# The experts' second matrix loaded with two neighbouring rows to a partition

## What is computed

```python
def expert_block(args):
    xb, e = args
    hid = xb @ w1[e] + b1[e]
    return clamped_swiglu(hid[:, :D_FF], hid[:, D_FF:]) @ w2[e] + b2[e]
```

## Time and profile before

| | before |
|---|---|
| median of 3 runs | 1869.51 us (1869.2 to 1870.19) |
| profiled execution, first to last instruction (span) | 1867.9 us |
| mean granted TensorE clock in it | 0.955 of 2.4 GHz |
| TensorE busy in the span | 1709.2 us (92%) |
| HBM read in it | 540.33 MB, of which the experts 384 loads of 1024 KB |
| expert loads under way | from 239.61 us to about 1222 us of the span |

### The profile page before, as it was taken

How to read it: one execution, slowest core, us unless ns; L and a number is a source line. 1 busy time by engine, 2 the same in 40 slices (tenths; PEclk the granted TensorE clock), 3 DMA queues, 4 the chain that set the end, 5 groups by cost and what they waited for, 6 DMA issues and landing times.

```text
span 1867.9 us, 20656 instructions
## 1 busy us (share of the span) xinstructions
PE 1709.2 (92%) x8372; PEld 1038.5 (56%) x8372; DVE 470.4 (25%) x1013; ACT 278.9 (15%) x572; POOL 131.5 (7%) x265
## 2 busy tenths in 40 slices
PE   6999999699967989598979789899999999999997
PEld 3644684144332534143434234377877888888886
DVE  4545422021111212021112112234566312121101
ACT  3114322011010111010011011022314300200000
POOL 5780000000000000000000000010003000000000
PEclk7999899899987989699999999999999999999999
DMA  9566089999999999999999999973443335525340
GB/s 377 184 234 229 25 353 370 397 413 414 418 421 416 412 419 419 420 414 412 418 422 416 413 419 418 407 290 113 157 159 113 113 114 202 203 90 180 117 176 24
DMA packets 134211, 547.03 MB, mean 293 GB/s; under 512 B 9195, under 2 KB 21111, under 8 KB 98268
## 3 DMA queue, kind: packets, MB, share of 16 engines
q1 hardware_dynamic: 129248, 529.83, 71.5%
q0 software_dynamic: 4128, 14.42, 2.1%
q10 hardware_dynamic: 732, 1.38, 0.2%
HBM read 540.33 MB, written 7.62 MB: 293 GB/s over the span
## 4 chain that ended last, share of the span: by engine, by line
PE 54%; DMA 15%; SPq 14%; issue 1%; DVE 0%; ACT 0%; DVEq 0%
SPq L1714 14%; PE PS L1337 10%; DMA arena<-in_w 9%; PE PS L2279 8%; DMA ring<-in_w 6%; PE PS L1362 5%; PE PS L2118 4%; PE PS L2305 4%; PE PS L2131 3%; PE PS L2139 3%; PE PS L1313 2%; PE PS L2125 2%; PE PS L1373 2%; PE PS L2269 2%; PE PS L2147 1%; PE PS L1347 1%
## 5 line engine op out<-in xcount | busy, mean ns | idle before, releaser
L1337 PE MATMUL PS<-ring,arena 128*64 128x512 f32 (+2 forms) x960 | 297.5, 672 | 58.0 <-DMA arena<-in_w 38.3
L1337 PE MATMUL PS<-arena 128*32 128x512 f32 (+2 forms) x968 | 269.9, 674 | 28.6 <-DMA ring<-in_w 20.3
L1337 PEld LDWEIGHTS PS<-ring,arena 128*64 128x64 f32 (+2 forms) x960 | 85.9, 141 | 204.2 <-issue 204.0
L1362 PE MATMUL PS<-ring,arena 128*64 128x512 f32 (+2 forms) x528 | 154.3, 620 | 12.5 <-DMA arena<-in_w 8.6
L1337 PEld LDWEIGHTS PS<-arena 128*32 128x32 f32 (+2 forms) x968 | 79.4, 141 | 137.5 <-issue 137.3
L2279 PE MATMUL PS<-arena,ring 128*128 128x256 f32 x704 | 152.6, 379 | 0.0
L1605 DVE TENSOR_SCALAR arena<-PS 128x512 f32<-128x512 f32 x28 | 19.3, 691 | 504.2 <-PE PS L1347 504.2
L2279 PEld LDWEIGHTS PS<-arena,ring 128*128 128x128 f32 x704 | 133.5, 190 | 18.0
L1362 PE MATMUL PS<-arena 128*32 128x512 f32 (+2 forms) x424 | 112.9, 630 | 23.1 <-DMA ring<-in_w 14.7
L1362 PEld LDWEIGHTS PS<-ring,arena 128*64 128x64 f32 (+2 forms) x528 | 47.5, 135 | 87.2 <-issue 86.2
L2118 PE MATMUL PS<-arena,ring 128*128 128x256 f32 x384 | 84.8, 380 | 0.0
(11 more groups left out here) (466 smaller groups left out, 2132.4 us busy)
## 6 DMA issues: line engine op xcount, KB each, us to landing
ring<-in_w SPq DMA_DIRECT2D x186, 1024.0 KB, 23.1
arena<-in_w SPq DMA_DIRECT2D x174, 1024.0 KB, 22.9
ring<-in_w_ada SPq DMA_DIRECT2D x24, 1024.0 KB, 9.5
cst<-in_w SPq DMA_DIRECT2D x24, 1024.0 KB, 23.8
ring<-in_w_in SPq DMA_DIRECT2D x22, 1024.0 KB, 7.3
ring<-in_w_up SPq DMA_DIRECT2D x20, 1024.0 KB, 8.9
ring<-in_w_gate SPq DMA_DIRECT2D x16, 1024.0 KB, 6.4
ring<-in_w_down SPq DMA_DIRECT2D x11, 1024.0 KB, 8.2
```

Of the source, the lines that this page charges most:

```text
L1337: m = pe.matmul(bank(("up", i, b))[rows[n], :], xs[:, k, rows[n]], tiles[n][:, b * 512:(b + 1) * 512], start=k == 0, stop=False, skip_grou ...
L1362: m = pe.matmul(bank(("down", i, c))[rows[n], :], actT[:, k, rows[n]], tiles[n][:, a:a + 512], start=k == 0, stop=k == 7, skip_group_check ...
```

## The change

A piece of `w2` is now read as one run: partition p gets rows 2p and 2p + 1 of the 256, which are neighbours in HBM, so 8 KB come in one piece and the DMA has the shape 128 x 2048 instead of 128 x 2 x 1024. The slot's half a now holds the rows 2p + a. So that the features still meet their rows, the transposes of a group of 256 features take every second column: even ones for the first half, odd ones for the second. The sums are the same.

```diff
 def __init__(self, slot, fill, after, src, m, n, rank=None, added=0):
-        self.added = added
+        self.added, self.paired = added, False
...
     def expert(self, key, src, m, n, rank, slot=None):
         self.weights[key] = (m, [self.load(src, m, n, rank, slot)])
+        self.loads[-1].paired = m > 1
...
                         for j in range(4):
-                            m = pe.transpose(bank(("flip", i, c), j * 128, (j + 1) * 128), um[c][:, j * 128:(j + 1) * 128], ident)
+                            half = um[c][:, j // 2 * 256:j // 2 * 256 + 256].rearrange("t (f a) -> t a f", a=2)
+                            m = pe.transpose(bank(("flip", i, c), j * 128, (j + 1) * 128), half[:, j % 2, :], ident)
...
-                    sp.dma_start(v, one.src.rearrange("(k p) n -> p k n", p=128)).then_inc(filled[one.slot], 16)
+                    if one.paired:
+                        sp.dma_start(v.rearrange("p k n -> p (k n)"), one.src.rearrange("(p k) n -> p (k n)", p=128)).then_inc(filled[one.slot], 16)
+                    else:
+                        sp.dma_start(v, one.src.rearrange("(k p) n -> p k n", p=128)).then_inc(filled[one.slot], 16)
...
-                    sp.dma_start(v, one.src[bass.ds(known[one.rank], 1), :, :].rearrange("e (k p) n -> p (e k) n", p=128)).then_inc(filled[one.slot], 16)
+                    src = one.src[bass.ds(known[one.rank], 1), :, :]
+                    if one.m > 1:
+                        sp.dma_start(v.rearrange("p k n -> p (k n)"), src.rearrange("e (p k) n -> p (e k n)", p=128)).then_inc(filled[one.slot], 16)
+                    else:
+                        sp.dma_start(v, src.rearrange("e (k p) n -> p (e k) n", p=128)).then_inc(filled[one.slot], 16)
```

## The result

The changed kernel takes 1859.13 us (median of four runs, 1855.82 to 1863.16) against 1869.36 us for the kernel before beside it (1868.87 to 1870.19): a ratio of 0.9943, with a 95% interval of 0.9926 to 0.996. The forecast was 1860.9 us with a range of 1859.2 to 1864.5; the median lies 1.8 us under the forecast and 0.07 us under the lower end of the range. The profiled execution is one of 1859.9 us, with a span of 1858.1 us and a mean granted clock of 0.961.

What follows compares the result with a forecast made beforehand. The prediction took the experts' stage to be bound by its stream of 384 loads. 126 `w2` loads at 0.069 us gave 8.6 us, transposes and stream loss zero: 1869.5 - 8.6 = 1860.9 us, range 1859.2 to 1864.5.

Steps and rivals of the forecast that it cites:

- neither grows nor shrinks: From 1226 us on, behind the experts' stage: TensorE's 642 us only move with the stage's end.
- The stage lasts as long as its loads: Experts' stage, to about 1225 us: its 384 loads set its length; TensorE waits 125.1 us for them.
- the 116 forecast: Experts' stage: TensorE's waits for DMA were to be near 125 - 9 = 116 us after the change.
- 126 x 0.069 = 8.6: Experts' stage: 126 `w2` loads each gain 0.069 us at `w1`'s rate, 8.6 us; upper bound 9.4, lower bound zero.
- I take no loss: At 420 to 470 us: the stream gets 1.5 us further ahead, within its 1.9 us margin; otherwise 7.1 us gained.
- a sign of being wrong: At about 420 to 470 us: a DMA share below 1 would show the prediction wrong.
- The likeliest case: Whole kernel: the forecast itself, 7.1 to 9.4 us gained, 1859.6 to 1862.9 us, chance 0.79.
- part of it: Stream runs dry where TensorE has no gap, or form explains only part of the rate: 1863 to 1866, chance 0.10.
- The end of the stage: Last `w2` matmuls: last eight loads come 0.55 us sooner, 0.84 of 1.39 us waiting stays; the end follows the last load.
- The transposes: Ahead of `down`, eight to a unit, 112 in all: reading every second column costs zero, at most 1.15 us a unit.
- my upper bound of 144 ns more: Weight load of a transpose, 128 columns, 141 ns before: most that the step of two could add, from line 500.
- The rule of line rate: Experts' loads: by the skill, full rate from 512 bytes on, so no gain, 1869.5 us; the windows disagreed.

Runs made afterwards that it cites:

- e1_again: The changed kernel as it is, timed again beside the kernel before: 1858.56 us, ratio 0.9944.
- e5_before_again: The kernel before, unchanged, timed against itself: 1868.39 us, ratio 1.0006.
- e3_load_only: The changed kernel with the old transposes, so only the loads are new: 1859.49 us, ratio 0.9952 of the kernel before.
- e4_half_units: Loads and transposes changed in units 0 to 6 only, the rest as in the kernel before: 1865.17 us, ratio 0.9977.
- e6_w1_4k: The changed kernel with `w1` of units 1 to 13 read as 256 pieces of 4 KB: 1878.31 us.
- e2_turn_only: The kernel before with the strided transposes alone and the old loads: 1867.0 us, ratio 0.9992.
- e10_pieces: Loads alone, all computing left out, `w1` streamed in sections: 387, 410, 422 and 428 GB/s at pieces of 2, 4, 8 and 16 KB.
- e7_w2_2k: The changed kernel with `w2` of units 1 to 13 read as 512 pieces of 2 KB: 1890.54 us.

## Why the prediction was right in its steps, and where it failed

**The step that failed** is the one that put the time outside the stage at a constant: what follows the stage "neither grows nor shrinks", the part ahead of it got no term at all, and the range allowed for "runs that spread by half a microsecond either way". That was read off three runs of the kernel before, 1869.2 to 1870.19. The runs showed something else. In the thirteen traces of kernels that run the same instructions there, the time outside the stage (the span less the stage) lies between 936 and 943 us, and behind the stage it goes with the granted clock, 632 to 636 us of TensorE's time. More runs of the kernel before lie between 1864.18 and 1872.85 (23 beside `e1_again`) and between 1864.12 and 1872.59 (24 beside `e5_before_again`): 3 to 5.5 us either way of the median. The changed kernel's own four span 7.3 us, and the fastest of them had a mean clock of 0.964, the slowest 0.956.

The scatter alone is not the whole of it. Three medians of the changed kernel, 1859.13, 1858.56 and 1857.99, all lie under the range. The mean of its 16 runs is 1858.8 us, that of the 90 runs of the kernel before on record 1868.9: 10.1 us less, by my estimate from the spread of the runs 8.9 to 11.3. The mean of 1858.8 is 2.1 us under the forecast of 1860.9: 0.6 us is the start at 1869.5, which three runs had put too high, and some 1.7 us are gain beyond the 8.4 of the traced stages, whose own gain is 0.2 short of its term. Whether the change itself wins this outside the stage stays open: the time there is 940.9 us in the mean of the three traces with the old loads and 938.4 in that of the four with the new ones, but single traces of either kind overlap. The mechanism, the sign and the term of the stage hold.

One reading of a row was off by a slice: the 397 GB/s that the prediction counts to the plateau are those of the eighth slice; from the ninth on it is 412 to 422. Nothing follows from it.

**The stage lasts as long as its loads.** Right: 8.4 us less in the mean of seven traces, and it moves with the length of the piece in every experiment, by +15.7 and +25.6 us with smaller ones. TensorE's waits for the loads, from 330 to 1225 us of after (total, times, longest; the last 11 us lie behind the stage), answer to the earlier trace rows:

```profile
PE PS L1338 <- DMA arena<-in_w: 50.9, 16, 6.3
PE PS L1338 <- DMA ring<-in_w: 42.2, 13, 6.3
PE PS L1363 <- DMA ring<-in_w: 16.4, 6, 5.6
PE PS L1363 <- DMA arena<-in_w: 13.4, 9, 5.6
```

They are 122.9 us, not the 116 forecast, but TensorE was also busy 6.9 us less in this stage (793.01 us against 799.93) at a mean clock of 0.94 instead of 0.93, and a TensorE that works faster waits more. Over the three traces with the old loads and the four with the new the waits are 129.0 and 119.8 us in the mean, 9.2 less. The ones ahead of `down`, 36.2 us before, are 29.4 to 30.1 in all four.

**126 x 0.069 = 8.6.** Right within what traces resolve: 8.4 in the mean, 9.25 in the pair that the prediction was about, of which the difference from 8.6 is within the bound of 9.4.

**"I take no loss" at 420 to 470 us.** Half right. Loads of line 1723 (`w1`) issued from 420 to 470 us, in after and in `e1_again`:

```profile
DMA to landing us min/median/max: 6.7/19.4/27.4
```

```profile
DMA to landing us min/median/max: 4.8/18.5/27.5
```

In after the fastest took 6.7 us, as in the earlier trace rows; I had expected 1.5 us less, so that trace had room. 4.8 us, as in `e1_again`, is what the fastest load of all took the earlier trace rows, so little or nothing was under way ahead of it. So in three traces of four the stream did pause and the DMA share fell below 1, which the prediction had named as a sign of being wrong; the cost, by the difference of the stages, is about 1.4 us, where the prediction had priced the loss at 1.5. The likeliest case and the rival *part of it* take turns, with TensorE's distance behind the stream, to which the granted clock adds 1.7 us in some runs. In size this is small beside the scatter of the runs.

**The end of the stage.** The wait ahead of the last `w2` matmuls is 0.17 us after, where 0.84 was forecast and 1.39 stood before; in `e1_again` and `e3_load_only` it is 0.17 and 0.19. It goes with the shape of the last `w2` loads: 1.38 in `e4_half_units`, whose last units have the old one, 0.17 in `e6_w1_4k`, whose `w2` has the new one. These matmuls start at 1210.19 us, not near 1213; 2.4 us of that are the stage's earlier start. The last eight loads came 1.2 us sooner against TensorE and not 0.55. Why is not traced; the end still follows the last load, but a stream any faster would hand the end of the stage to TensorE.

**The transposes.** Zero was right for the time and wrong for the instruction. After, line 1383 (ns min/median/max), answering to the earlier trace rows:

```profile
L1383 PEld LDWEIGHTS PS<-cst,arena x112: 194/209/222, 328.8 to 1198.4; 128*128 128x128 f32 x112
L1383 PE MATMUL PS<-cst,arena x112: 272/283/386, 328.8 to 1198.5; 128*128 128x128 f32 x112
```

The weight load takes 209 ns instead of 141, half of the way to my upper bound of 144 ns more. By the Trainium skill, "SBUF — State Buffer", section "Specifications (TRN2)", two floats within 16 bytes are read at full rate; the weight load of this trace disagrees by 68 ns for 128 columns. Most of it lies beside the matmuls: 8 x 68 ns are 0.54 us, but eight transposes take 1.11 us, not 1.04, and this is hidden in TensorE's waits (`e2_turn_only`).

**The rule of line rate.** By the Trainium skill, "DMA: Bandwidth & Descriptors", section "Specifications", all of these pieces are long enough for full rate; 387, 410, 422 and 428 GB/s at 2, 4, 8 and 16 KB disagree. The Trainium skill's figure of 3 cycles for a packet ("DMA: Bandwidth & Descriptors", section "Why small descriptors are slow (HBM only)") gives the right sign but less than half of the size: 1.2% by the prediction's estimate from it, 2.7 to 2.9% by the windows.

## What to carry to other kernels

Where the windows show a stage in which the DMA share is 1 and TensorE waits for loads, look at the longest run of bytes that each load reads: going from 8 KB to 4 KB pieces cost 2.8% of the rate here, and on to 2 KB another 5.6%, and choosing which rows share a partition cost no time here, where the other operand could be turned to match. Before a range of a few tenths of a per cent is given, find how far runs of the unchanged kernel lie apart; three that agree say little, and parts in which nothing is changed move too. And read the place where a faster stream would run out of room: it is the next limit, and it came up here at once.

## What the hardware showed that I had not expected

**The price is one for each piece.** 1.0486 MB take 2.71, 2.56, 2.485 and 2.45 us at 2, 4, 8 and 16 KB, an estimate from the rates of `e10_pieces`. That is 2.41 us plus 0.54 to 0.6 ns for each of 512, 256, 128 and 64 pieces, so the step from 8 KB to 16 KB is worth 0.035 us a load, half of this one. It wasn't tried in the kernel, whose slots hold 8 KB to a partition.

**Fewer pieces let the queue reach further ahead.** The loads after, in part 6 of the page, answer to the earlier trace rows:

```profile
ring<-in_w SPq DMA_DIRECT2D x186, 1024.0 KB, 26.3
arena<-in_w SPq DMA_DIRECT2D x174, 1024.0 KB, 26.2
cst<-in_w SPq DMA_DIRECT2D x24, 1024.0 KB, 27.1
```

Each load moves sooner and yet takes 26 us to land instead of 23. With smaller pieces it takes less, 18.6 to 20.4 us in `e6_w1_4k` and 20.5 to 21.0 in `e7_w2_2k`, so the loads are issued less far ahead. `e10_pieces` shows that the queue does this by itself, with no engine to free a slot: its code allows eight loads under way in every section. Line 49, its loads, from 40 to 160 us (2 KB pieces) and from 380 to 480 us (8 KB pieces), with the time of the issuing instruction in ns:

```profile
L49 SPq DMA_DIRECT2D ring<-in_w x45: 1131/2583/4629, 36.6 to 157.7; - x45
DMA to landing us min/median/max: 14.2/14.4/16.2
```

```profile
L49 SPq DMA_DIRECT2D ring<-in_w x40: 327/328/328, 381.6 to 478.7; - x40
DMA to landing us min/median/max: 19.9/19.9/19.9
```

With 8 KB pieces all eight loads are under way (8 x 2.485 = 19.9 us), the issue takes 0.33 us, and SyncE waits for a load to land (85.7 of the 100 us). With 2 KB pieces SyncE never waits for one, the issue itself takes 2.6 us, and only 14.4 / 2.71 = 5.3 loads are under way. With 4 KB pieces it is 18.5 / 2.56 = 7.2. So the room is not a number of loads, and fewer pieces make more loads fit. It is no fixed number of pieces either: 5.3 x 512 is some 2700, 7.2 x 256 some 1850. What the queue counts stays open.
